# Two decoder layers on one core: the loop over layers written out, one weight tile split earlier, and the last norm writing its output directly

## The chip, the cores and the metric

One Trainium2 chip, of which the kernel uses one core. The metric is the device time of the whole program in microseconds. A core has five engines with their own instruction queues: TensorE (PE, matmuls, with weight loads shown apart as PEld), VectorE (DVE), ScalarE (ACT), GpSimd (POOL) and SyncE (SP), which here only issues transfers. They meet through semaphores.

## What is computed

Two layers of a causal decoder over 512 tokens of width 1024, all in float32. For each layer:

```
h = x @ w_in                       # split into three mixers and three gates
x = layer_norm(ALPHA * x + merged @ w_out)                     # norm 1
f_gate, f_up = split(x @ w_ffn_in)
ffn = (silu(f_gate) * f_up) @ w_ffn_out
ple = sigmoid(x @ w_ple_gate) * (p_i @ w_ple_proj)
x = layer_norm(ALPHA * x + ffn + ple)                          # norm 2
```

The mixers are sparse attention over the best 128 keys, latent attention, and a gated causal convolution of width 31. The result is x after the second layer.

## The kernel before

**Data.** Activations lie with features on the 128 partitions: `x` is eight blocks (`DK = 8`) of 128x512. To multiply in nearly full float32 precision, each operand is split into a high half (rounded to fp32r) and a low half (the rest), and each product is three matmuls: high by high, high by low, low by high (`three`, and the loop of `group`). The residual stream is kept as `xh` and `xl`.

**Weights.** Each layer's weights are 152 tiles (`TILES`) of 128x1024. SP loads tile t into `wraw` (two slots, `load`), ACT rounds it into `wh` (`high`, four slots, `WS`), POOL subtracts to make `wl` (`low`), and PE waits for `lo_ready` (`arrived`). SP may load a tile when the low half of the tile two before is made. ACT may write a slot of `wh` when PE has used the tile four before. ACT's queue is written out by hand: `high(n + LEAD)` with `LEAD = 3` stands beside the use of tile n, so that when a layer ends the first three tiles of the next one are split. The fourth (tile 3) is asked for at the head of the next pass of the layer loop, `high(n + LEAD, first)` at n = 0, that is behind everything that ACT does for norm 2. `weights` holds three tiles more than the two layers have, so that the last pass can load ahead as well; SP, ACT and POOL handle these three too.

**The layer loop.** ACT, PE, DVE and POOL each run `Fori(0, L)`, a hardware loop with the layer number in a register; semaphore counts that depend on it are worked out by register instructions. Within it stand shorter hardware loops (the 22 passes over the FFN's input tiles, for one).

**Norm 2 and the layer's end.** `norm` on DVE adds the last blocks, PE forms mean and mean square (L938, L946), ACT takes the root (`deviation`), and PE spreads the scale over the partitions (L950). Then, for each block j, DVE centres it (L1282) and scales it (L1306, signals `z_ready`); ACT adds the bias and rounds it into `xh` (`norm_high`, L579, signals `x_high`); DVE makes `xl` (L1312, signals `x_ready`). After norm 2 of either layer DVE also adds `xh` and `xl` back together into `u` (L1316, signals `z_full`). The next layer's first four tiles (group "idx", two blocks of x each, 24 matmuls each) start with `x_ready` of block 0. After the second layer, ACT sends `u` to `out` in four transfers of two blocks, each on `z_full`, behind its last `norm_high`.

Of the kernel before, what the change touches and what calls it, by code (L numbers as in the profile page):

```python
# [19 lines left out]
ALU = mybir.AluOpType  # L20
ACT = mybir.ActivationFunctionType
F32 = mybir.dt.float32
# [6 lines left out]
L = 2  # L29
NT = S // P  # L30
DK = D // P
# [46 lines left out]
T_PP = T_OUT + DK  # L78
T_PG = T_PP + 4
T_FI = T_PG + DK  # L80
T_FO = T_FI + 2 * FK
PARTS = -(-FK // DK)
TILES = T_FO + PARTS * DK
assert TILES % 4 == 0
TILE = 1024
LEAD = 3
WS = 4
# [135 lines left out]
def build(nc, x_t, ple_t, pos, freq, weights, params, out):  # L223
    with ExitStack() as ctx:
# [5 lines left out]
        def sem(name):  # L230
# [3 lines left out]
        xh = sb("xh", 0, [P, DK, S], F32R)  # L234
        xl = sb("xl", 16384, [P, DK, S], F32R)
        wraw = sb("wraw", 32768, [P, 2, TILE])
# [8 lines left out]
        par = sb("par", 78848, [P, NPAR])  # L245
        praw = sb("praw", 79680, [P, 2, S])
# [50 lines left out]
        u = sb("u", A0 + 90112, [P, DK, S])  # L297
# [26 lines left out]
        raw_loaded = [sem("raw_loaded0"), sem("raw_loaded1")]  # L324
        hi_ready, lo_ready, tile_used = sem("hi_ready"), sem("lo_ready"), sem("tile_used")
# [5 lines left out]
        par_loaded, ple_loaded, out_stored = sem("par_loaded"), sem("ple_loaded"), sem("out_stored")  # L331
# [26 lines left out]
        z_ready, x_high, x_ready, z_full = (  # L358
            sem("z_ready"), sem("x_high"), sem("x_ready"), sem("z_full"))
# [20 lines left out]
        def column(name, j):  # L380
            return par[:, PAR[name] + j:PAR[name] + j + 1]
# [4 lines left out]
        @block.sync  # L386
        def _(sp):
            for t in range(2):
                sp.dma_start(wraw[:, t, :], weights[t]).then_inc(raw_loaded[t], 16)
            def load(t, tile):  # L390

                sp.wait_ge(lo_ready, tile - 1)
                sp.dma_start(wraw[:, t, :], weights[bass.ds(tile, 1)].rearrange("a p n -> (a p) n")).then_inc(
                    raw_loaded[t], 16)

            with sp.Fori(1, L * TILES // 2 + 1) as m:
                for t in range(2):
                    load(t, m * 2 + t)
            sp.wait_ge(lo_ready, L * TILES + 1)
            sp.dma_start(wraw[:, 0, :], weights[L * TILES + 2]).then_inc(raw_loaded[0], 16)  # L400


        @block.gpsimd
        def _(pool):

            nc.gpsimd.memset(ident[:], 0.0).then_inc(zeroed, 1)
            nc.gpsimd.memset(causal[:], 0.0).then_inc(zeroed, 1)
            nc.gpsimd.memset(ones_d[:], 1.0 / D).then_inc(consts_ready, 1)
            nc.gpsimd.memset(ones_c[:], 1.0 / CC).then_inc(consts_ready, 1)
            nc.gpsimd.memset(ones_1[:], 1.0).then_inc(consts_ready, 1)  # L410
            nc.gpsimd.memset(eps_ln, LN_EPS).then_inc(consts_ready, 1)
            nc.gpsimd.memset(small[:, 64:72], 0.0).then_inc(consts_ready, 1)
            nc.gpsimd.memset(small[:, 76:128], 0.0).then_inc(consts_ready, 1)
            pool.wait_ge(zeroed, 2)
            nc.gpsimd.affine_select(out=ident[:], in_=ident[:], compare_op=ALU.not_equal, fill=1.0, base=0,
                                    pattern=[[-1, P]], channel_multiplier=1).then_inc(consts_ready, 1)
            nc.gpsimd.affine_select(out=causal[:, S - P:S], in_=causal[:, S - P:S], compare_op=ALU.is_ge, fill=NEG,
                                    base=0, pattern=[[-1, P]], channel_multiplier=1).then_inc(consts_ready, 1)

            def low(t, first):  # L420

                pool.wait_ge(hi_ready, first + (t + 1))  # L422
                nc.gpsimd.tensor_tensor(wl[:, t % WS, :], wraw[:, t % 2, :], wh[:, t % WS, :].bitcast(F32),  # L423
                                        ALU.subtract).then_inc(lo_ready, 1)

            for t in range(LEAD):
                low(t, 0)
            pool.sem_inc(passed, 1)
            with pool.Fori(0, L) as layer:
                first = layer * TILES  # L430
                with pool.Fori(0, T_PP // 4) as i:  # L431
                    for k in range(4):
                        low(LEAD + k, first + i * 4)
                with pool.Fori(0, (TILES - T_PP) // 4) as i:  # L434
                    for k in range(4):
                        low(T_PP + LEAD + k, first + i * 4)

        def logit(n):

# [4 lines left out]
        tile_group, t, col = {}, 0, {}  # L444
        for g, (name, ncol, nk, tiles) in enumerate(TOKEN_GROUPS):
# [4 lines left out]
            if t == T_CONV:  # L450
                t = T_U
# [4 lines left out]
        def _(act):  # L456
# [17 lines left out]
            def high(t, first):  # L474

                act.wait_ge(tile_used, first + (max(t - (WS - 1), 0) + START))
                act.wait_ge(raw_loaded[t % 2], first * 8 + 16 * (t // 2 + 1))
                nc.scalar.activation(wh[:, t % WS, :], wraw[:, t % 2, :], ACT.Copy).then_inc(hi_ready, 1)  # L478
# [98 lines left out]
            def norm_high(layer, n, j):  # L577
                act.wait_ge(z_ready, layer * 16 + (8 * n + j + 1))
                nc.scalar.activation(xh[:, j], u[:, j], ACT.Identity,  # L579
                                     bias=column(("l1b", "l2b")[n], j)).then_inc(x_high, 1)  # L580

            for t in range(LEAD):
                high(t, 0)
            with act.Fori(0, L) as layer:
                first = layer * TILES
                for kind, n in FRONT:
                    if kind == "tile":
                        high(n + LEAD, first)
                        if n == 1:

                            act.wait_ge(x_ready, layer * 16 + DK)
                            act.dma_start(par[:], params[bass.ds(layer, 1)].rearrange("a p n -> (a p) n")).then_inc(
                                par_loaded, 16)
                            act.dma_start(praw[:], ple_t[bass.ds(layer, 1)].rearrange("a p k n -> (a p) k n")).then_inc(
                                ple_loaded, 16)
                        if n in tile_group:
                            g, k = tile_group[n]
                            name, ncol, _, tiles = TOKEN_GROUPS[g]
# [6 lines left out]
                        elif CONV_PLACE[n][1] == 0:  # L605
                            j = CONV_PLACE[n][0]
# [59 lines left out]
                for q in range(12):  # L666
# [7 lines left out]
                    if q >= 8:  # L674
                        for c in range(2):
                            n = 2 * (q - 8) + c
# [40 lines left out]
                        nc.scalar.activation(hh[:, bass.ds(i * 2 + c, 1), :].rearrange("p a n -> p (a n)"),  # L717
                                             th[:, c, :], ACT.Copy, scale=0.5).then_inc(ffn_high, 1)
                for k in range(PARTS * DK):
                    high(T_FO + k + LEAD, first)  # L720
                    j = k // PARTS
                    if k % PARTS == 0 and j >= 4:
                        for jj in range(4) if j == 4 else range(j - 1, j):
                            squares(layer, 1, jj)
                squares(layer, 1, DK - 1)
                deviation(layer, 1)
                for j in range(DK):
                    norm_high(layer, 1, j)
            for j in range(0, DK, 2):
                act.wait_ge(z_full, (L - 1) * DK + j + 2)  # L730
                act.dma_start(out[:, j:j + 2], u[:, j:j + 2]).then_inc(out_stored, 16)
            act.wait_ge(out_stored, 16 * 4)


        @block.tensor
        def _(pe):
# [232 lines left out]
            pe.sem_inc(tile_used, START)  # L969
            pe.wait_ge(consts_ready, 8)  # L970
            pe.sem_inc(passed, 1)
            with pe.Fori(0, L) as layer:
                first = layer * TILES
                for kind, n in FRONT:
                    if kind == "scratch":
# [95 lines left out]
        def _(dve):  # L1071
# [152 lines left out]
            def norm(layer, n, start, tile):  # L1224
# [2 lines left out]


                x0, g, b = layer * 16 + 8 * n, ("l1g", "l2g")[n], ("l1b", "l2b")[n]
                total, squares = sums[n][:, 0], sums[n][:, 1]  # L1230

                def arrive(j):
# [66 lines left out]
                    center(j)  # L1299
                steps.wait()  # L1300
                dve.wait_ge(spread, layer * 2 + (n + 1))
                for j in range(DK + 2):
                    if j < DK:
                        if j >= EARLY:
                            steps.wait(back=min(EARLY - 1, DK - 1 - j))
                        v.scalar_tensor_tensor(u[:, j], u[:, j], column(g, j), scale, ALU.mult,  # L1306
                                               ALU.mult).then_inc(z_ready, 1)
                        if j + EARLY < DK:
                            center(j + EARLY)
                    if 1 <= j <= DK:  # L1310
                        dve.wait_ge(x_high, x0 + (DK + j))
                        v.scalar_tensor_tensor(xl[:, j - 1], u[:, j - 1], column(b, j - 1), xh[:, j - 1].bitcast(F32),  # L1312
                                               ALU.add, ALU.subtract).then_inc(x_ready, 1)
                    if n == 1 and j >= 2:
                        dve.wait_ge(x_ready, x0 + (DK + j - 1))
                        v.tensor_tensor(u[:, j - 2], xh[:, j - 2].bitcast(F32), xl[:, j - 2].bitcast(F32),  # L1316
                                        ALU.add).then_inc(z_full, 1)

            dve.sem_inc(passed, 1)
            with dve.Fori(0, L) as layer:  # L1320
                first = layer * TILES
                steps.stage(layer * V_LAYER)
                dve.wait_ge(par_loaded, layer * 16 + 16)
# [307 lines left out]
```

## Time and profile before

| what | value |
|---|---|
| median of three runs | 1975.85 us (1975.3 to 1978.69) |
| the profiled execution, its own time | 1980.51 us |
| its span, first to last instruction | 1978.7 us |
| mean granted TensorE clock | 0.979 |
| PE busy | 1873.0 us, 95% of the span |
| ACT, DVE, POOL busy | 37%, 51%, 38% |

Times in the trace are microseconds from the start of the span. PE's share of busy time counts matmuls that overlap in the pipeline, so it is no measure of how near PE is to its best, but where PE is idle the row says how long and for whom.

### The profile page before, as it was taken

The page shows a single profiled execution, that of the slowest core. Times are in us where ns is not written, and L with a number is a line of the kernel's source. Part 1 is how long each engine was busy: PE and PEld are TensorE (multiplying, and loading weights), DVE is VectorE, ACT ScalarE, POOL GpSimd, SP SyncE. Part 2 cuts the span into 40 slices and gives each one's busy share as a digit, 9 for nine tenths or more (in the row PEclk, how much of TensorE's full clock was granted, in tenths as well). Part 3 has the DMA queues.
Part 4 walks back from the last instruction along what each step waited for, and adds up shares of the span by engine and source line. Part 5 has one row for each costly group of instructions (what it writes and reads, how often), then busy time and mean ns, then how long its engine had stood idle before and what let it go on. Part 6 is the DMA issues. An engine that isn't in the chain of part 4 may idle for free.

```text
span 1978.7 us, 27887 instructions
## 1 busy us (share of the span) xinstructions
PE 1873.0 (95%) x9048; PEld 1551.4 (78%) x9048; DVE 1002.4 (51%) x1898; ACT 737.5 (37%) x1256; POOL 752.4 (38%) x321
## 2 busy tenths in 40 slices
PE   6999999999999999999999999999999899999995
PEld 5877878878777888887787878888777788888873
DVE  3269667748974111112353876676588721111025
ACT  3443455543342222222244435555433422222222
POOL 4433222234444444443443422222353534444441
PEclk9999999999999999999899999999999999999997
DMA  5222111112222222232232211111132222222322
GB/s 164 95 76 85 54 50 57 55 57 93 96 96 85 95 95 95 96 106 85 97 99 85 97 65 52 46 54 65 61 101 85 97 95 95 95 95 96 106 96 75
DMA packets 46334, 167.86 MB, mean 85 GB/s; under 512 B 5392, under 2 KB 5648, under 8 KB 46224
## 3 DMA queue, kind: packets, MB, share of 16 engines
q1 hardware_dynamic: 44208, 160.98, 24.6%
q10 hardware_dynamic: 2016, 5.47, 0.8%
q8 instruction: 62, 1.02, 0.2%
q14 instruction: 48, 0.39, 0.1%
HBM read 164.33 MB, written 2.10 MB: 84 GB/s over the span
## 4 chain that ended last, share of the span: by engine, by line
issue 68%; POOL 27%; PE 2%; DVE 1%; POOLq 1%; ACT 0%; DMA 0%; DVEq 0%; ACTq 0%
POOL sb_wl L423 27%; PE banks L741 1%; PE banks L739 1%; PE banks L740 1%; POOLq L422 0%; POOLq L434 0%; POOLq L431 0%; DVE sb_xl L1312 0%; DMA sb_rope_tmp<-in_freq 0%; DVE sb_u L1306 0%; ACT sb_xh L471 0%; DVE sb_u L1282 0%; PE banks L938 0%; PE banks L946 0%; PE banks L950 0%
## 5 line engine op out<-in xcount | busy, mean ns | idle before, releaser
L423 POOL TENSOR_TENSOR sb_wl<-sb_wraw,sb_wh 128x1024 fp32r<-128x1024 f32 x307 | 750.4, 2448 | 1194.1 <-ACT sb_wh L478 1193.8
L739 PE MATMUL banks<-sb_xh,sb_wh 128*128 128x512 f32 x1344 | 553.4, 412 | 12.2 <-DVE sb_u L1510 9.1
L741 PE MATMUL banks<-sb_xh,sb_wl 128*128 128x512 f32 x1344 | 529.0, 394 | 0.0
L740 PE MATMUL banks<-sb_xl,sb_wh 128*128 128x512 f32 x1344 | 528.7, 393 | 0.0
L478 ACT ACTIVATE sb_wh<-sb_wraw 128x1024 fp32r<-128x1024 f32 x307 | 323.2, 1055 | 271.0 <-PE banks L741 167.2
L739 PEld LDWEIGHTS banks<-sb_xh,sb_wh 128*128 128x128 f32 x1344 | 255.8, 190 | 62.4 <-POOL sb_wl L423 11.7
L741 PEld LDWEIGHTS banks<-sb_xh,sb_wl 128*128 128x128 f32 x1344 | 254.7, 190 | 54.8
L740 PEld LDWEIGHTS banks<-sb_xl,sb_wh 128*128 128x128 f32 x1344 | 256.2, 191 | 40.6
L1175 DVE SCALAR_TENSOR_TENSOR banks<-sb_hconv,sb_par,banks 128x512 f32<-128x512 f32 x232 | 173.8, 749 | 0.5
L739 PE MATMUL banks<-sb_hh,sb_wh 128*128 128x512 f32 x352 | 138.9, 395 | 1.6 <-POOL sb_wl L423 1.6
L741 PE MATMUL banks<-sb_hh,sb_wl 128*128 128x512 f32 x352 | 138.0, 392 | 0.0
L740 PE MATMUL banks<-sb_hl,sb_wh 128*128 128x512 f32 x352 | 137.4, 390 | 0.0
L1234 DVE TENSOR_TENSOR sb_u<-sb_u,banks 128x512 f32<-128x512 f32 x32 | 21.9, 686 | 198.8 <-PE banks L741 197.7
L1522 DVE TENSOR_TENSOR sb_th<-sb_th,banks 128x512 f32<-128x512 f32 x44 | 30.2, 687 | 181.3 <-PE banks L741 181.3
L783 PE MATMUL banks<-sb_wh,sb_xh 128*128 128x452 f32 (+3 forms) x256 | 91.5, 357 | 25.2 <-POOL sb_wl L423 21.8
L1519 DVE SCALAR_TENSOR_TENSOR sb_th<-sb_th,banks 128x512 f32<-128x512 f32 x44 | 30.3, 688 | 167.2 <-ACT sb_th L482 167.2
L523 ACT ACTIVATE sb_ptbuf<-banks 128x128 f32<-128x128 f32 (+3 forms) x128 | 55.8, 436 | 143.4 <-PE banks L839 143.3
L482 ACT ACTIVATE sb_th<-banks 128x512 f32<-128x512 f32 x60 | 35.9, 598 | 192.4 <-PE banks L741 192.1
L717 ACT ACTIVATE sb_hh<-sb_th 128x512 f32 x44 | 27.8, 632 | 207.7 <-DVE sb_th L1522 207.7
L784 PE MATMUL banks<-sb_wl,sb_xh 128*128 128x452 f32 (+3 forms) x256 | 90.9, 355 | 0.0
L785 PE MATMUL banks<-sb_wh,sb_xl 128*128 128x452 f32 (+3 forms) x256 | 90.6, 354 | 0.0
L739 PEld LDWEIGHTS banks<-sb_hh,sb_wh 128*128 128x128 f32 x352 | 66.1, 188 | 16.9 <-POOL sb_wl L423 2.5
(266 smaller groups left out, 2872.2 us busy)
## 6 DMA issues: line engine op xcount, KB each, us to landing
sb_wraw<-in_weights SPq DMA_DIRECT2D x307, 512.0 KB, 3.3
sb_u<-in_x ACTq DMA_DIRECT2D x4, 512.0 KB, 7.4
out<-sb_u ACTq DMA_DIRECT2D x4, 512.0 KB, 3.6
sb_praw<-in_ple ACTq DMA_DIRECT2D x2, 512.0 KB, 4.4
sb_par<-in_params ACTq DMA_DIRECT2D x2, 98.5 KB, 2.6
sb_rope_tmp<-in_freq ACTq DMA_DIRECT2D x1, 24.0 KB, 5.0
sb_small<-in_pos ACTq DMA_DIRECT2D x1, 2.0 KB, 3.8
```

Of the source, the lines that this page charges most:

```text
L423: nc.gpsimd.tensor_tensor(wl[:, t % WS, :], wraw[:, t % 2, :], wh[:, t % WS, :].bitcast(F32), ALU.subtract).then_inc(lo_ready, 1)
L478: nc.scalar.activation(wh[:, t % WS, :], wraw[:, t % 2, :], ACT.Copy).then_inc(hi_ready, 1)
L482: nc.scalar.activation(dst, psum[:, bank, :], ACT.Tanh, scale=0.5, bias=bias).then_inc(done, 1)
L523: nc.scalar.activation(ptbuf[:, n % 2, 0:w], psum[:, bank, 0:w], ACT.Copy).then_inc(turn_out, 1)
L739: nc.tensor.matmul(out, wh_, xh_, start=start, stop=False)
L740: nc.tensor.matmul(out, wh_, xl_, start=False, stop=False)
L741: return nc.tensor.matmul(out, wl_, xh_, start=False, stop=stop)
L783: nc.tensor.matmul(o, th_, h[:, kk], start=(k == 0), stop=False)
L784: nc.tensor.matmul(o, th_, lw[:, kk], start=False, stop=False)
L785: last = nc.tensor.matmul(o, tl_, h[:, kk], start=False, stop=(k == nk * tiles - 1))
L1175: steps.done(v.scalar_tensor_tensor(acc, h, w, acc, ALU.mult, ALU.add))
L1519: steps.done(v.scalar_tensor_tensor(tc, tc, 1.0, psum[:, 4 + 2 * c, :], ALU.add, ALU.mult))
```

## The change

Four things. The layer loop of ACT, PE and DVE becomes a Python loop, so its body stands twice in each engine's program with constants in place of the register; POOL runs one flat loop over all tiles. At the end of layer 0, `high` of the next layer's tile 3 is issued between `deviation` and the eight `norm_high`, and dropped at n = 0 of layer 1. The three tiles past the end are no longer loaded nor split. In norm 2, L1316 is gone from both layers; in the last layer L1312 is gone too, and ACT's Identity adds the bias and writes the float32 value straight to `u`, each block signals `z_full`, and SP (no longer ACT) sends each block by itself, eight transfers of 256 KB.

```diff
@@ sync
-            with sp.Fori(1, L * TILES // 2 + 1) as m:
+            with sp.Fori(1, L * TILES // 2) as m:
                 for t in range(2):
                     load(t, m * 2 + t)
-            sp.wait_ge(lo_ready, L * TILES + 1)
-            sp.dma_start(wraw[:, 0, :], weights[L * TILES + 2]).then_inc(raw_loaded[0], 16)
+            for j in range(DK):
+                sp.wait_ge(z_full, j + 1)
+                sp.dma_start(out[:, j], u[:, j]).then_inc(out_stored, 16)
+            sp.wait_ge(out_stored, 16 * DK)
@@ gpsimd
-            for t in range(LEAD):
-                low(t, 0)
             pool.sem_inc(passed, 1)
-            with pool.Fori(0, L) as layer:
-                first = layer * TILES
-                with pool.Fori(0, T_PP // 4) as i:
-                    for k in range(4):
-                        low(LEAD + k, first + i * 4)
-                with pool.Fori(0, (TILES - T_PP) // 4) as i:
-                    for k in range(4):
-                        low(T_PP + LEAD + k, first + i * 4)
+            with pool.Fori(0, L * TILES // WS) as i:
+                for k in range(WS):
+                    low(k, i * WS)
@@ scalar
-            with act.Fori(0, L) as layer:
+            for layer in range(L):
                 first = layer * TILES
                 for kind, n in FRONT:
                     if kind == "tile":
-                        high(n + LEAD, first)
+                        if layer == 0 or n > 0:
+                            high(n + LEAD, first)
...
                 for k in range(PARTS * DK):
-                    high(T_FO + k + LEAD, first)
+                    if T_FO + k + LEAD < TILES or layer < L - 1:
+                        high(T_FO + k + LEAD, first)
...
                 deviation(layer, 1)
-                for j in range(DK):
-                    norm_high(layer, 1, j)
-            for j in range(0, DK, 2):
-                act.wait_ge(z_full, (L - 1) * DK + j + 2)
-                act.dma_start(out[:, j:j + 2], u[:, j:j + 2]).then_inc(out_stored, 16)
-            act.wait_ge(out_stored, 16 * 4)
+                if layer < L - 1:
+                    high(LEAD, first + TILES)
+                    for j in range(DK):
+                        norm_high(layer, 1, j)
+                else:
+                    for j in range(DK):
+                        act.wait_ge(z_ready, layer * 16 + (DK + j + 1))
+                        nc.scalar.activation(u[:, j], u[:, j], ACT.Identity,
+                                             bias=column("l2b", j)).then_inc(z_full, 1)
@@ tensor
-            with pe.Fori(0, L) as layer:
+            for layer in range(L):
@@ vector, norm
+                last = n == 1 and layer == L - 1
-                for j in range(DK + 2):
+                for j in range(DK + 1):
...
-                    if 1 <= j <= DK:
+                    if 1 <= j <= DK and not last:
                         dve.wait_ge(x_high, x0 + (DK + j))
...
-                    if n == 1 and j >= 2:
-                        dve.wait_ge(x_ready, x0 + (DK + j - 1))
-                        v.tensor_tensor(u[:, j - 2], xh[:, j - 2].bitcast(F32), xl[:, j - 2].bitcast(F32),
-                                        ALU.add).then_inc(z_full, 1)
@@ vector
-            with dve.Fori(0, L) as layer:
+            for layer in range(L):
@@ kernel
-    tiles = np.concatenate([tiles, tiles[:LEAD]], axis=0)
```

## Rows read from the trace of the kernel before

**Rows 1.** The page: span and instructions of all queues, and each engine's busy time.
```profile
span 1978.7 us, 27887 instructions
PE 1873.0 (95%) x9048; PEld 1551.4 (78%) x9048; DVE 1002.4 (51%) x1898; ACT 737.5 (37%) x1256; POOL 752.4 (38%) x321
```

**Rows 2.** Waits of PE: engine, tile, line <- releaser: us in total, times, longest.
```profile
PE banks L783 <- POOL sb_wl L423: 21.8, 2, 18.4
PE banks L839 <- DVE sb_ystage L1160: 16.2, 20, 1.4
...
PE banks L811 <- DVE sb_cl L1354: 6.7, 2, 3.4
```

**Rows 3.** Timeline of ACT, the layer boundary: start, us, what [idle before <- releaser].
```profile
983.87 0.72 ACT L579 ACTIVATE sb_xh<-sb_u,sb_par 128x512 fp32r<-128x512 f32 x1 [3.96 <-DVE sb_u L1306]
...
1001.72 1.28 ACT L478 ACT_TABLE_LOAD   x1 [1.95 <-issue]
...
1003.02 2.00 ACT L478 ACTIVATE sb_wh<-sb_wraw 128x1024 fp32r<-128x1024 f32 x2
```

**Rows 4.** Timeline of PE at the boundary, around tile 3's start and end.
```profile
1002.99 0.36 PE L785 MATMUL banks<-sb_wh,sb_xl 128*128 128x452 f32 x1
1006.71 0.47 PE L783 MATMUL banks<-sb_wh,sb_xh 128*128 128x452 f32 x1 [3.36 <-POOL sb_wl L423]
...
1012.71 0.37 PE L783 MATMUL banks<-sb_wh,sb_xh 128*128 128x452 f32 x1
...
1013.32 0.35 PE L783 MATMUL banks<-sb_wh,sb_xh 128*128 128x416 f32 x1
```

**Rows 5.** Stretches: length, busy us (x instructions) by engine, PEclk, DMA share, GB/s.
```profile
991.00:1003.00 12.00, 12.00 (x61) 10.99 (x59) 11.15 (x18) 4.18 (x5) 0.00 (x0) 1.00 0.01 2
1008.20:1011.20 3.00, 3.00 (x9) 2.63 (x9) 0.00 (x0) 0.21 (x1) 0.72 (x1) 0.50 0.79 264
103.00:110.00 7.00, 5.79 (x16) 4.74 (x17) 3.62 (x6) 1.63 (x2) 2.37 (x1) 0.52 0.01 2
1076.80:1083.80 7.00, 5.83 (x28) 4.82 (x28) 3.54 (x6) 1.64 (x2) 2.39 (x1) 1.00 0.01 2
```

**Rows 6.** Timeline of all engines, norm 2 of layer 0, its DVE steps.
```profile
980.15 0.69 DVE L1294 TENSOR_TENSOR sb_sums<-sb_ident,sb_small 128x512 f32<-128x512 f32 x1
...
985.61 0.75 DVE L1312 SCALAR_TENSOR_TENSOR sb_xl<-sb_u,sb_par,sb_xh 128x512 fp32r<-128x512 f32 x1
```

**Rows 7.** Timelines of ACT, POOL and DVE in norm 1 of layer 0.
```profile
546.69 1.04 ACT L478 ACTIVATE sb_wh<-sb_wraw 128x1024 fp32r<-128x1024 f32 x1
...
547.81 2.36 POOL L423 TENSOR_TENSOR sb_wl<-sb_wraw,sb_wh 128x1024 fp32r<-128x1024 f32 x1 [6.45 <-ACT sb_wh L478]
...
555.54 2.03 DVE L1312 SCALAR_TENSOR_TENSOR sb_xl<-sb_u,sb_par,sb_xh 128x512 fp32r<-128x512 f32 x1
```

**Rows 8.** Timeline of DVE and ACT, last layer's norm 2.
```profile
1955.62 0.75 DVE L1306 SCALAR_TENSOR_TENSOR sb_u<-sb_u,sb_par,banks 128x512 f32<-128x512 f32 x1 [0.54 <-PE banks L950]
...
1961.32 0.74 DVE L1306 SCALAR_TENSOR_TENSOR sb_u<-sb_u,sb_par,banks 128x512 f32<-128x512 f32 x1
1961.98 0.68 DVE L1282 TENSOR_TENSOR sb_u<-sb_u,banks 128x512 f32<-128x512 f32 x1
...
1962.58 0.74 DVE L1312 SCALAR_TENSOR_TENSOR sb_xl<-sb_u,sb_par,sb_xh 128x512 fp32r<-128x512 f32 x1
...
1963.84 0.74 DVE L1306 SCALAR_TENSOR_TENSOR sb_u<-sb_u,sb_par,banks 128x512 f32<-128x512 f32 x1
```

**Rows 9.** Timeline of DVE, the last pieces.
```profile
1973.39 1.28 DVE L1316 TENSOR_TENSOR sb_u<-sb_xh,sb_xl 128x512 f32<-128x512 f32 x2
```

**Rows 10.** The source view of the output transfers, L731.
```profile
L731 ACTq DMA_DIRECT2D out<-sb_u x4: 338/404/557, 1971.7 to 1974.7; - x4
...
DMA to landing us min/median/max: 2.7/3.6/4.3
```

**Rows 11.** The DMA view from 1970 us to the end, rate in 40 equal slices.
```profile
GB/s 0 0 0 0 0 0 0 0 0 0 0 255 400 400 364 455 400 364 437 400 400 419 346 437 419 419 382 400 401 419 437 400 364 455 146 0 0 0 0 0
```

More of the change, by code:

```diff
@@ L587, in _ @@
                     if kind == "tile":
-                        high(n + LEAD, first)
+                        if layer == 0 or n > 0:
+                            high(n + LEAD, first)
                         if n == 1:
                             act.wait_ge(x_ready, layer * 16 + DK)
-                            act.dma_start(par[:], params[bass.ds(layer, 1)].rearrange("a p n -> (a p) n")).then_inc(
+                            act.dma_start(par[:], params[layer]).then_inc(
                                 par_loaded, 16)
-                            act.dma_start(praw[:], ple_t[bass.ds(layer, 1)].rearrange("a p k n -> (a p) k n")).then_inc(
+                            act.dma_start(praw[:], ple_t[layer]).then_inc(
                                 ple_loaded, 16)
```

## The prediction

> **What bounds the kernel now.** I read the page first [rows 1]: PE is busy for 1873.0 of 1978.7 us. The change takes nothing from PE's work, so it can only win where PE is idle or after PE has ended. The view of waits shows who keeps PE idle [rows 2]. The line to see is PE L783 waiting for POOL's low half, 21.8 us in two waits: one of 18.4 us is the start of the program, which the change leaves alone; the other is 3.4 us. I then looked at two places in the timelines, the layer boundary and the end.
>
> At the boundary, PE starts layer 1 when DVE has made block 0 of `xl` at 985.61 + 0.75 = 986.36 us [rows 6], and then runs without a gap through tiles 0 to 2 (61 matmuls in 12 us, clock 1.00, the faster of its two levels, 2.4 GHz) [rows 5]. Tile 3 is not there: its first matmul is at 1006.71, 3.72 us after the one before [rows 4]. ACT is why. It has ended its last `norm_high` at 1001.72 - 1.95 = 999.77, is then 1.95 us idle for nothing but issue (the head of the loop), loads a table for 1.28 us, and only at 1003.02 rounds tile 3 [rows 3]; POOL's low half of it comes after that, and PE's idle time ends with it [rows 4]. Behind the gap PE's granted clock is 0.50 (1.2 GHz) in the stretch 1008.2 to 1011.2, where only 9 matmuls pass in 3 us [rows 5].
>
> At the end PE has nothing left once it has spread the scale, and from 1955.62 on the last 23 us are one chain on DVE, then the transfers: scale, centre, `xl`, and the sum back into `u` for each block, 2.52 us a block (scale at 1961.32, the next at 1963.84) [rows 8]. The last sum ends at 1973.39 + 1.28 = 1974.67, ACT issues the last transfer right behind it (L731's last start is 1974.7), and it takes about 3.6 us to land; 0.4 us of closing remain to 1978.7 [rows 9, 10]. ACT's first transfer could not leave before 1971.7, as it stands behind the last `norm_high`, so 2 MB go out at about 400 GB/s in 5.2 us: the queue is full from the first issue to the end [rows 11].
>
> **Part 1: tile 3 split ahead of the norm's high halves.** The moved instructions are one `high` of 1.06 us (L478) on ACT and, through it, one `low` of 2.4 us on POOL (2.36 at 547.81 [rows 7]), and SP's load of tile 5, which waits for that low half. The edit takes them past the eight `norm_high` in ACT's queue; POOL has nothing else in its queue and SP only the later loads, which come earlier too. ACT is idle for 3.96 us between the root and block 0's `norm_high` (979.91 to 983.87) [rows 3]. The `high` would run from about 979.9 to 980.9, POOL from 980.95 to 983.35. Even with a table load of 1.28 us ahead of it ACT would be free at 982.3, so nothing behind it is late. Its own waits are met: the slot is free when the down projection has ended, and the raw tile has been there since before the norm. Norm 1 already has this order and shows it: `high` at 546.69 behind the root, with no table load between, `low` at 547.81 [rows 7]. PE then finds tile 3 ready at 1003.2.
>
> What PE gains: it passes from tile 2's last start (1002.99) to tile 4's first (1013.32) in 10.33 us [rows 4]. At the pitch of the full clock, 0.203 us (three steps from 1012.71 to 1013.32), these 25 steps take 5.1 us. The gain is 5.2 us: 3.5 us of idle time and 1.7 us that the half clock costs. What is late next? Tile 4: after the last `norm_high` (now near 996.8, since DVE drops L1316, 0.60 us a block [rows 8]) ACT rounds it at once, and POOL has it by about 1000.2, 8 us before PE asks at 1008.1. Block 7 of `xl` is there by 997.6, wanted after 1005. So no new wait, 5.2 us stay.
>
> The neighbour that speaks against it is POOL beside DVE. L1312, with two inputs in SBUF, takes 0.74 us alone and 2.03 us where a `low` ran beside it (555.54) [rows 6, 7]. At the boundary the only such instruction near the moved `low` is L1294, at 980.15 to 980.84; the `low` comes in 0.1 us after it ends, and 0.8 us after it has begun. The first L1312 is at 985.61, 2.2 us after the `low` [rows 6]. I charge nothing; were the `low` to start first and L1294 to wait for the whole of it, all that follows would be 2.4 us later and part 1 worth 2.8 us. The Trainium skill (SBUF — State Buffer, section SBUF: two separate sides) says that GpSimd and a VectorE instruction with two SBUF inputs take a shared port pair in turn, the first to start for its whole length; the rows of norm 1 agree. By that rule the order of the two starts decides between the two sums, and as they start now it is the first.
>
> **Part 2: the end.** On DVE, per block, the 0.66 us from L1312's start to L1316's and the 0.60 us from there to the next scale go, 1962.58 to 1963.84. What stays is 0.66 us from scale to centre and 0.60 from the centre to what follows, 1.26 us (1961.32 to 1962.58) [rows 8]. Scale 0 starts at 1955.62 as now; scale 6 at 1955.62 + 6 x 1.26 = 1963.18; scale 7 follows 0.66 us later at 1963.84 and ends at 1964.58. ACT's Identity (0.72 us, as L579 [rows 3]; f32 output, taken as equal) ends at 1965.33 and keeps up, 0.72 in 1.26. SP, free since its last load, issues within 0.04 us. Landing of 256 KB is not in the trace. Above it lies the fastest 512 KB transfer, 2.7 us [rows 10]; below it that less 256 KB at 400 GB/s [rows 11], 2.1 us. The transfers are 1.26 us apart, more than the 0.65 us each needs at 400 GB/s, so they don't queue unless 2 KB rows go at half the rate; then one takes 1.3 us and the last is late by about 0.3 us. I take 2.3 us. The end is 1965.37 + 2.3 + 0.4 = 1968.1, a gain of 10.6 us, between 9.9 and 10.8. The Trainium skill (DMA: Bandwidth & Descriptors, section Anatomy of one DMA) gives 2.0 us plus the bytes at 436 GB/s for a transfer of another path; as an estimate that is 2.6 us here and a gain of 10.3 us, and no run so far shows a transfer of this size.
>
> **Part 3: the layers written out, three tiles fewer.** The loop head's 1.95 us and table load on ACT are in part 1. The three extra tiles are split beside down-projection matmuls that don't wait for them: nothing. The page counts 27,887 instructions, 21,571 of them in the busy rows [rows 1]; the other 6,300 are register, semaphore, branch and issue instructions, and most of the register ones go. They mostly run while their engine is busy with the instruction before. They can count only where PE waits on another engine's reply: 20 waits on L1160 of 0.8 us, above all [rows 2]. If none is on such a path the gain is 0; the trace's rows don't price a register step, so from above I take a quarter of the 16.2 us of those 20 waits, 4 us. I take 1 us, nearer to nothing, since the steps in [rows 8] follow one another before the one ahead has fully ended, with no room for a register step between them. Twice as much program as a body is the same instructions streamed as now, since each layer passes through its body once.
>
> **Sum.** 5.2 + 10.6 + 1.0 = 16.8 us: the profiled execution of 1980.51 us (span 1978.7 and 1.8 around it) would become 1963.7. The median of the runs is 4.7 us under the profiled one; with the same 16.8 us off it is 1959.0. A measurement of this kernel can tell about 0.2%, 4 us, from no change.
>
> **Rivals.**
> - *The clock takes some of it back.* PE's granted clock after a gap isn't steady: an idle time of 3.4 us before L811, once in each layer (6.7 us in two), is followed by half clock in layer 0 (16 matmuls in 7 us) and by full clock in layer 1 (28) [rows 2, 5]. Everything in layer 1 moves by 5 us, so that gap may fall the other way: 12 matmuls x 0.25 us (7 / 28) = 3.0 us lost, giving 1962.0, or half that if only the boundary's 1.7 us stay. It can win as much elsewhere. Chance 0.15.
> - *POOL holds DVE at the boundary*, as above: 2.4 us, 1961.4. The margin of 0.8 us speaks against it. Chance 0.04.
> - *The boundary edit does nothing for the time*: tile 4 or the parameter transfer becomes the late one and takes the place of tile 3. Then 10.6 + 1 stay: 1964.2. POOL's 2.4 us a tile against PE's 4.9 speaks against it. Chance 0.04.
> - *The register instructions count in full*: 3 us more, 1956. Chance 0.10.
> - *Slower*: instruction fetch of the written-out program. A jump to code that isn't at hand costs ACT 1.95 us [rows 3]. If the straight program stalled PE like that at the borders of fetched blocks, 9 such stalls (17.6 us) eat the gain, from 11 on it is slower by 0.2%, and 12 give 1982.4. Against it: the body is already this straight, and 61 matmuls pass without a gap [rows 5]. Chance 0.05, of which 0.02 for 7 to 10 stalls, within 0.2%.
>
> The forecast has the other 0.62, with its own range 1957 to 1961.5. Range for 8 in 10: 1954.5 (register gain in full and a kinder clock) to 1965 (boundary edit void, transfers at the slow bound). Faster by over 0.2%: 0.95; within: 0.02; slower: 0.03.
>
> **What would show it.** Part 1: L478 between L575 and the first L579, one `low` before 984 us, no idle on PE L783 for POOL but the start's, no half clock near 1008 us; tile 4's first matmul near 1008.1 us. Part 2: L1306 at 1.26 us pitch, the last transfer 9.7 us after the first L1306, the span's end about 12.5 us after it instead of 23.1. Part 3: PE's waits on L1160 a little shorter. It is wrong if PE shows a new wait near tile 4, if L1294 or L1312 takes over 2 us there, or if PE gets short gaps that no engine explains.

## The result, and the profile after

The changed kernel takes 1967.09 us (median of five runs, 1966.31 to 1967.98), the kernel before 1975.85 us in the same job (five runs, 1975.16 to 1979.2): ratio 0.995, interval 0.9937 to 0.9962. It is faster by 8.8 us where 16.8 were forecast, and it lies above the range. The profiled execution took 1966.31 us; its span is 14.2 us shorter than that of [rows 1]. The page:

```profile
span 1964.5 us, 25834 instructions
PE 1874.9 (95%) x9048; PEld 1553.1 (79%) x9048; DVE 992.2 (51%) x1874; ACT 730.1 (37%) x1250; POOL 745.6 (38%) x318
```

PE has as many matmuls as before and is busy 1.9 us longer. The waits of PE (as [rows 2]):

```profile
PE banks L783 <- POOL sb_wl L425: 18.1, 1, 18.1
PE banks L839 <- DVE sb_ystage L1160: 14.5, 20, 1.3
...
PE banks L811 <- DVE sb_cl L1351: 6.9, 2, 3.4
```

L783 waits for POOL once, at the start; the 3.4 us wait at the boundary is gone. The 20 waits on L1160 are 1.7 us shorter together. Further down, two waits of 1.5 us before L783 now have no releaser ("issue", 3.1 us in two); in the kernel before the same two stand as waits for ACT (3.0 us in two), so they are no new gaps.

**The boundary**, as [rows 3] and [rows 6]. Timeline of ACT:

```profile
978.80 0.30 ACT L570 ACTIVATE sb_small<-sb_small 128x4 f32<-128x4 f32 x1 [0.85 <-DVE sb_small L1291]
979.00 1.04 ACT L473 ACTIVATE sb_wh<-sb_wraw 128x1024 fp32r<-128x1024 f32 x1
982.97 0.72 ACT L574 ACTIVATE sb_xh<-sb_u,sb_par 128x512 fp32r<-128x512 f32 x1 [2.92 <-DVE sb_u L1307]
...
995.13 0.72 ACT L574 ACTIVATE sb_xh<-sb_u,sb_par 128x512 fp32r<-128x512 f32 x1 [0.60 <-DVE sb_u L1307]
995.76 1.05 ACT L473 ACTIVATE sb_wh<-sb_wraw 128x1024 fp32r<-128x1024 f32 x1
```

Timelines of DVE, POOL and PE, and PE's stretch over tiles 2 to 4:

```profile
979.34 0.69 DVE L1295 TENSOR_TENSOR sb_sums<-sb_ident,sb_small 128x512 f32<-128x512 f32 x1
...
984.70 0.74 DVE L1313 SCALAR_TENSOR_TENSOR sb_xl<-sb_u,sb_par,sb_xh 128x512 fp32r<-128x512 f32 x1
```

```profile
980.12 2.35 POOL L425 TENSOR_TENSOR sb_wl<-sb_wraw,sb_wh 128x1024 fp32r<-128x1024 f32 x1 [5.63 <-ACT sb_wh L473]
996.89 4.76 POOL L425 TENSOR_TENSOR sb_wl<-sb_wraw,sb_wh 128x1024 fp32r<-128x1024 f32 x2 [14.42 <-ACT sb_wh L473]
```

```profile
985.59 0.71 PE L783 MATMUL banks<-sb_wh,sb_xh 128*128 128x452 f32 x1 [3.52 <-DVE sb_xl L1313]
```

```profile
1001.00:1007.00 6.00, 6.00 (x31) 5.51 (x30) 0.00 (x0) 1.06 (x1) 2.87 (x2) 1.00 0.53 167
```

ACT rounds tile 3 right behind the root, without a table load, and tile 4 with no gap behind its last `norm_high`. POOL makes the low half just after L1295 has ended, and both DVE instructions keep their 0.7 us. PE runs through at the faster clock, with no idle time and no half clock at 1008.

**The end**, as [rows 8] to [rows 10]. Timelines of DVE, then ACT, then SP's queue, and the source view of the transfers:

```profile
1952.38 0.75 DVE L1307 SCALAR_TENSOR_TENSOR sb_u<-sb_u,sb_par,banks 128x512 f32<-128x512 f32 x1 [0.55 <-PE banks L950]
1953.05 0.68 DVE L1283 TENSOR_TENSOR sb_u<-sb_u,banks 128x512 f32<-128x512 f32 x1
1953.64 0.74 DVE L1307 SCALAR_TENSOR_TENSOR sb_u<-sb_u,sb_par,banks 128x512 f32<-128x512 f32 x1
...
1959.92 1.40 DVE L1307 SCALAR_TENSOR_TENSOR sb_u<-sb_u,sb_par,banks 128x512 f32<-128x512 f32 x2
```

```profile
1953.16 0.72 ACT L731 ACTIVATE sb_u<-sb_u,sb_par 128x512 f32<-128x512 f32 x1 [3.97 <-DVE sb_u L1307]
...
1960.70 1.38 ACT L731 ACTIVATE sb_u<-sb_u,sb_par 128x512 f32<-128x512 f32 x2 [0.53 <-DVE sb_u L1307]
```

```profile
L401 SPq DMA_DIRECT2D out<-sb_u x8: 332/332/349, 1953.9 to 1962.1; - x8
...
DMA to landing us min/median/max: 2.0/2.0/2.1
```

The scales are 1.26 us apart, as forecast, and the Identity takes 0.72. A transfer of 256 KB lands in 2.0 us where the prediction took 2.3. From the first scale to the end of the span it is 12.1 us, from 23.1.

**Where it came back.** So each mended place gained what it should. Part of the time was lost where nothing was changed: in norm 1, and behind the gap at L811. As [rows 5], first 12 us around norm 1 of layer 1 in the kernel before, then the same in the changed one and 7 us from the gap at L811 of its layer 1:

```profile
1514.00:1526.00 12.00, 10.09 (x43) 7.30 (x42) 8.23 (x16) 4.84 (x8) 2.56 (x2) 0.86 0.27 89
```

```profile
1508.00:1520.00 12.00, 10.50 (x37) 7.21 (x36) 6.32 (x12) 3.36 (x5) 3.39 (x2) 0.72 0.24 70
1071.00:1078.00 7.00, 5.81 (x21) 4.82 (x22) 3.59 (x6) 1.63 (x2) 2.39 (x1) 0.76 0.00 0
```

PE's timeline of the changed kernel at both places shows what half clock (1.2 GHz) is:

```profile
1072.19 0.93 PE L811 MATMUL banks<-sb_ident,sb_h_ckv 128*128 128x128 f32 x4 [3.42 <-DVE sb_cl L1351]
...
1073.35 0.63 PE L740 MATMUL banks<-sb_xl,sb_wh 128*128 128x512 f32 x1
1073.77 0.63 PE L741 MATMUL banks<-sb_xh,sb_wl 128*128 128x512 f32 x1
...
1511.37 2.39 PE L938 MATMUL banks<-sb_ones_d,sb_sums 128*128 128x1 f32 x16 [1.50 <-DVE sb_sums L1271]
...
1515.90 0.63 PE L740 MATMUL banks<-sb_pl,sb_wh 128*128 128x512 f32 x1
1516.33 0.63 PE L741 MATMUL banks<-sb_ph,sb_wl 128*128 128x512 f32 x1
```

The matmuls stand 0.42 us apart instead of 0.23, though the idle times ahead of them are no longer than before (3.4 us at L811 in both kernels, 1.5 us at norm 1 of layer 1 where it was 1.9). I laid the two traces side by side by the number of the matmul (both kernels have the same 9048 in the same order) and took the time from one to another:

| between matmuls | where | before | after |
|---|---|---|---|
| 96 to 2668 | layer 0 up to norm 1 | 505.88 | 505.21 |
| 2668 to 2677 | norm 1, layer 0 | 2.05 | 3.56 |
| 2677 to 4512 | layer 0 behind norm 1 | 430.04 | 429.50 |
| 4512 to 4524 | norm 2, layer 0 | 8.95 | 8.13 |
| 4524 to 4620 | layer 1, tiles 0 to 3 | 26.92 | 21.96 |
| 4700 to 5000 | around L811, layer 1 | 57.59 | 59.14 |
| 5300 to 7182 | attention and output, layer 1 | 378.05 | 376.71 |
| 7182 to 7208 | norm 1, layer 1 | 6.08 | 7.58 |
| 7208 to 9000 | layer 1 behind norm 1 | 417.99 | 418.53 |
| last matmul to the end | | 24.26 | 13.32 |

Two norms and L811 give back 1.5 + 1.5 + 1.6 = 4.6 us.

### The profile page after: what moved, and what is told of

Same layout as the page of the kernel before. It is cut to its first block, busy times and chain, and to the rows that moved or that the text cites. A ratio compares the mean times of both kernels' runs of the same rounds, so it can differ in the third digit from the quotient of the medians.

```text
span 1964.5 us, 25834 instructions
## 1 busy us (share of the span) xinstructions
PE 1874.9 (95%) x9048; PEld 1553.1 (79%) x9048; DVE 992.2 (51%) x1874; ACT 730.1 (37%) x1250; POOL 745.6 (38%) x318
## 4 chain that ended last, share of the span: by engine, by line
issue 68%; POOL 28%; PE 2%; POOLq 1%; DVE 0%; ACT 0%; DVEq 0%
POOL sb_wl L425 28%; PE banks L739 1%; PE banks L741 1%; PE banks L740 1%; POOLq L424 0%; POOLq L429 0%; DVE sb_u L1307 0%; DVE sb_u L1283 0%; PE banks L938 0%; PE banks L946 0%; PE banks L950 0%; POOLq L425 0%; ACT sb_u L731 0%; DVE sb_sums L1271 0%; DVE sb_u L1235 0%
## 5 line engine op out<-in xcount | busy, mean ns | idle before, releaser
L783 PE MATMUL banks<-sb_wh,sb_xh 128*128 128x452 f32 (+3 forms) x256 | 90.8, 355 | 21.6 <-POOL sb_wl L425 18.1
```

The costliest lines, as they stand in the source:

```text
L783: nc.tensor.matmul(o, th_, h[:, kk], start=(k == 0), stop=False)
```

## The experiments

Times are medians; "before" is that of the same job. The kernel before was run 66 times in all, with e1: 1973.96 to 1983.1, median 1978.0, mean 1977.9; the changed one 11 times with e5: 1963.7 to 1968.1, mean 1966.5. So the gain over many executions is near 11.4 us; the two jobs that hold both kernels gave 8.8 and 14.6.

**e1: the kernel before, unchanged.** For the spread of one program.

> The kernel before, unchanged, for more executions and another profile. Theory A (the profiled execution of before was one of its long ones, about 5 us over its usual time, and the sum was made against it): most executions at 1975 to 1976 and some at 1979 to 1980, the profile of a short one shows PE's pass over the boundary (tile 2's last start to tile 4's first) at 10.3 us as before and the missing 4 to 5 us somewhere in the middle, in stretches of half clock. Theory B (a part is worth less in the usual executions than in the profiled one): the pass over the boundary is shorter than 10.3 us, or the end after the first scale shorter than 23.1 us, in the short executions.

1976.06 us (12 runs, 1973.96 to 1982.14), before 1978.15, ratio 0.9992 [0.9981, 1.0002]. Its profiled span is 1974.8 us, 3.9 under [rows 1] for the same program, and the matmul-by-matmul comparison puts it in four places: norm 1 of layer 1 (6.08 to 4.59 us), 0.40 just ahead of it, 1.0 behind, and 1.14 in the last norm. The pass over the boundary (26.99 us) and the end (24.26) are as in the first trace, as Theory A expected. Its stretch there:

```profile
1514.00:1526.00 12.00, 10.49 (x51) 7.94 (x50) 9.71 (x19) 6.64 (x11) 2.95 (x2) 1.00 0.26 88
```

Clock 1.00 where the first trace had 0.86 and the changed kernel 0.72. The 0.40 are no clock: PE waited 1.9 us for the sums of norm 1 in the first trace and 1.5 here. The other 3.6 are where the half clock falls. The recorded clocks say the same of the runs that were not profiled: of 61 executions of this kernel, the 10 with a mean clock of 0.979 took 1981.9 us on average, the 23 with 0.982 took 1975.2.

**e2, e3, e4: one part at a time.** e2 only writes the layers out; e3 adds the boundary edit; e4 is e2 with the end's edits (L1316 gone from both layers, the last layer written by blocks) but without the move.

```diff
# e2
-            with act.Fori(0, L) as layer:
+            for layer in range(L):
# the same for PE and DVE
# e3 = e2 and
-                        high(n + LEAD, first)
+                        if layer == 0 or n > 0:
+                            high(n + LEAD, first)
...
+                if layer < L - 1:
+                    high(LEAD, first + TILES)
```

> Only the layer loops of ACT, PE and DVE written out; order, last norm, transfers and POOL's loops as before. The prediction's part 3 says 1 us faster, 1974.9. Theory A with a price for writing out (half clock falls differently, or fetch): 1979 to 1981, about 4 to 5 us slower than before. Theory B: 1974 to 1976.

> Written out as in the run before this one, and tile 3 of the next layer split ahead of the norm's high halves; last norm and transfers as before. Both theories take the difference to the written-out kernel: prediction 5.2 us less, 1969.7; Theory A: 5 us less than the written-out kernel, so 1975 to 1976, no gain over before; Theory B, boundary worth less: within 2 us of the written-out kernel.

> Written out, and the last norm writes full values and is sent block by block by SP; the sum back into u is gone from both layers; tile 3 stays behind the norm's high halves. Prediction: 10.6 us less than the written-out kernel, 1964.3. Theory A: also 10.6 us less than it, so 1969 to 1971. Theory B, end worth less: 6 us less than it or fewer.

e2: 1978.06 us (11 runs, 1970.47 to 1979.51), ratio 0.9994 [0.9981, 1.0008]. e3: 1977.42 (12, 1973.6 to 1979.27), 0.9993 [0.9982, 1.0004]. e4: 1965.96 (6, 1963.08 to 1968.15), 0.9937 [0.9922, 0.9951]; before 1978.15. e2 lies between what its two theories expected, e3 at 0.6 us under e2 where 5 were expected by Theory A (Theory B had named under 2, because the boundary would be worth less, which e3's trace below does not bear out), and e4 at 12.1 us under e2 where 10.6 were. By the medians the written-out loop and the boundary edit are worth nothing, and all of the gain is e4's edits'. Yet in e3's trace the boundary is 5.3 us shorter (tiles 0 to 3: 21.58 us for 26.92), and norm 1 of layer 1 takes 7.75 us for 6.08. The same is seen in e2 (7.85) and e4 (7.64). Already e2 mends most of the boundary; ACT there:

```profile
999.65 0.72 ACT L579 ACTIVATE sb_xh<-sb_u,sb_par 128x512 fp32r<-128x512 f32 x1 [1.20 <-DVE sb_u L1306]
1000.28 1.99 ACT L478 ACTIVATE sb_wh<-sb_wraw 128x1024 fp32r<-128x1024 f32 x2
```

Written out, ACT has neither the 1.95 us of the loop head nor the table load of 1.28 us of [rows 3] between the last `norm_high` and tile 3. Tile 3 starts 17.9 us behind layer 1's first matmul instead of 20.3, and PE's gap there is 1.4 us instead of 3.4. L1316 has a second part in what is left: with it in place POOL's low half of tile 3, which starts beside DVE's last sums, takes 3.57 us in e2 (3.54 in e9 below), and without it 2.40 in e4. That is the prediction's neighbour the other way round, POOL slowed beside a DVE instruction with two SBUF inputs.

**e5, e6: the changed kernel again, and with tile 3 left where it was** (behind the `norm_high`).

```diff
-                        if layer == 0 or n > 0:
-                            high(n + LEAD, first)
+                        high(n + LEAD, first)
...
-                    high(LEAD, first + TILES)
```

> The changed kernel, unchanged, beside the same executions of before as the three runs below. If the 1975.85 of before was a lucky small sample, the difference of the medians is 11 us; if not, 8 to 9 us as first measured.

> The changed kernel with tile 3 split behind the norm's high halves again, as in before. The prediction charges the move with the whole 5.2 us of the boundary: this would be 1972. The traces of the parts say that the loop head, the table load and the sum back into u alone made tile 3 late, and all three are gone anyway: then this is within 1 us of the changed kernel, and PE has no gap at tile 3.

e5: 1966.07 us, 0.9928 [0.9916, 0.994]; e6: 1967.45, 0.9932 [0.992, 0.9944]; before 1980.71. ACT in e6:

```profile
997.50 0.73 ACT L574 ACTIVATE sb_xh<-sb_u,sb_par 128x512 fp32r<-128x512 f32 x1 [0.59 <-DVE sb_u L1305]
998.13 1.04 ACT L473 ACTIVATE sb_wh<-sb_wraw 128x1024 fp32r<-128x1024 f32 x1
```

PE has no idle time there between 987.96 and 1010 us and its time for tiles 0 to 3 is 21.27 us. With the loop written out and L1316 gone, ACT is done with norm 2 early enough for tile 3 where it was: the move isn't needed. That is what was expected, and not the 1972 of the prediction's reading. e5's expectation named 11 us if the first sample of before was a lucky one, and 8 to 9 if not; its job gave 14.6.

**e7, e8: the clock held up.** To take the clock out of the comparison, that is to keep it at its faster level, PE gets work that nobody reads in the places where it waits: transposes of `ident` into a bank that is free there, 147 in each layer, in the kernel before (e7) and in the changed one (e8).

```diff
+            def keep(bank, n):
+                for _ in range(n):
+                    nc.tensor.transpose(psum[:, bank, 0:P], ident[:], ident[:])
# 26 ahead of L811's wait, 22 ahead of the first scores, 15 ahead of
# the sums of each norm, 9 more in norm 2, 34 behind norm 2, 26 ahead of the FFN
```

> The kernel before with transposes of the identity into a free PSUM bank issued by PE in its idle stretches (ahead of the fourth low half of the normed c, of the first score, of the norm's sums and spread, behind norm 2 and ahead of the FFN), about 130 a layer, nothing else changed. Clock theory (stretches of half clock behind PE's idle times cost both kernels some 8 to 14 us, and a different share in each execution): fewer stretches of half clock, 5 to 12 us faster than before, a narrower spread than 1974 to 1983. Rival (the clock is not what parts the executions): within 2 us of before, same spread, or slower by the fillers' length.

> The changed kernel with the same fillers. Clock theory (the change's steps give about 18 us: boundary 5, end 11, register steps 2, and moved stretches of half clock take 6 to 8 of them back): 16 to 18 us under the filled kernel before. Rival (the written-out program costs 5 us or more by fetch or otherwise): 10 to 12 us under it, as without fillers.

e7: 1960.98 us, 0.991 [0.9894, 0.9925]; e8: 1941.0, 0.9806 [0.9793, 0.9818]; before 1980.71. Both gained more than was expected: e7 is 19.7 us under before where 5 to 12 were named, and e8 is 20.0 under e7 where 16 to 18 were. e7's five runs lie between 1960.17 and 1961.18 but for one of 1966.59, whose mean clock is 0.993 where the others have 0.995 and 0.996. The rows of 100 to 1930 us, of before, after, e7 and e8 in this order, have the clock ahead of the DMA share:

```profile
100.00:1930.00 1830.00, 1767.97 (x8521) 1459.72 (x8520) 943.42 (x1794) 681.94 (x1168) 697.58 (x286) 0.99 0.25 83
```

```profile
100.00:1930.00 1830.00, 1772.64 (x8532) 1463.57 (x8531) 945.89 (x1787) 678.85 (x1166) 699.96 (x286) 0.98 0.26 83
```

```profile
100.00:1930.00 1830.00, 1792.46 (x8843) 1487.14 (x8842) 954.93 (x1799) 685.96 (x1173) 705.78 (x289) 1.00 0.25 84
```

```profile
100.00:1930.00 1830.00, 1798.62 (x8889) 1491.56 (x8887) 954.43 (x1802) 682.46 (x1172) 700.31 (x286) 1.00 0.26 83
```

The two figures of 1.00 are rounded: one short stretch of half clock is left in either trace, in e8 in norm 1 of layer 0 (2.72 us there, 1.84 in e12 below), in e7 behind a wait of 1.5 us in layer 1:

```profile
1090.00:1096.00 6.00, 5.75 (x37) 5.76 (x38) 5.69 (x17) 1.06 (x2) 2.38 (x1) 0.72 0.22 66
```

The fillers also move PE's start of layer 1 in e7: its jump to the loop head comes behind the 34 fillers, and PE starts 2.00 us after them, though block 0 of `xl` (made from 976.03 on) would have allowed it at 976.8. Timeline of PE in e7:

```profile
973.23 3.87 PE L739 MATMUL banks<-sb_ident 128*128 128x128 f32 x34
979.10 0.47 PE L787 MATMUL banks<-sb_wh,sb_xh 128*128 128x452 f32 x1 [2.00 <-DVE sb_xl L1325]
```

Norm 2 takes 9.55 us there and 7.37 in e8. e9's expectation counts this as a cost of the fillers, but it costs nothing: PE then waits for tile 3 anyway, 2.96 us, and tile 3's time is set by ACT (which rounds it at 993.44, behind its own loop head and table load) and POOL. Its first matmul comes 20.3 us behind block 0 of `xl` in e7, and 20.4 in the kernel before, where PE started at once.

So the parts with the clock held up are best read from the traces of e7 and e12 (the changed kernel without the move, below; its PE has no half clock while it is busy). The spans differ by 19.5 us: norm 2 and tiles 0 to 3 of layer 1 together 5.4 (32.52 to 27.11), the end 10.9 (23.78 to 12.85), attention of layer 0 1.6, e7's leftover half clock 1.6; the rest cancels out. Without the leftover 17.9 us are the change's, against 16.8 of the sum and near 11.4 with the clock free. e8 is also the fastest kernel: 25.5 us below the changed one although it issues 294 more matmuls. That fits an estimate from the changed kernel's trace: its clock records show half clock during 56 us of PE's busy time, of which half, 28 us, is lost.

**e9 to e12: the parts with the clock held up.** e9, e10 and e11 are e2, e3 and e4 with the fillers, e12 is e6 with them. e9 also tries the rival of instruction fetch with nothing else in its way.

> The layer loops written out, nothing else, with the fillers. The filled kernel before took 1961.0, of which 2.3 us are the fillers' own (PE's jump to the loop's head now comes behind them). Parts at a held clock: the jump's 2.3, 2.2 to 2.7 us of PE's 3.2 us gap at tile 3 (loop head and table load on ACT gone), about 2 us of register steps: 1954 to 1955. If writing out costs time by itself: 1958 or more.

> As the run before, and tile 3 split ahead of the norm's high halves, with the fillers. The prediction's whole boundary gain as the move's own: 5 us less than written out alone. The traces so far: only the last 0.5 to 1 us of the gap at tile 3 is left for it: 0.5 to 1 us less.

> Written out, the last norm's full values sent block by block, the sum back into u gone, with the fillers. At a held clock: 10.9 us for the end and the same 0.5 to 1 us at tile 3, since the norm's high halves end 3 us earlier without the sum: 11.5 to 12 us less than written out alone, 1942 to 1943. If the end is worth 10.6 us and no more, 10.6 us less.

> The changed kernel with tile 3 split behind the high halves again, with the fillers: the move alone, in the final kernel. Same as the filled changed kernel, 1941.0 within 0.5 us, if the move has nothing left to win; 1944 to 1946 if it has the gap.

| kernel | median us (range) | ratio to before, 1977.06 |
|---|---|---|
| e9, written out | 1956.06 (1955.1 to 1958.73) | 0.989 [0.9873, 0.9907] |
| e10, and boundary | 1952.11 (1951.76 to 1954.94) | 0.9876 [0.9858, 0.9894] |
| e11, e9 and end | 1941.49 (1941.01 to 1943.13) | 0.9819 [0.9805, 0.9834] |
| e12, e8 without the move | 1941.12 (1940.8 to 1941.49) | 0.9817 [0.9802, 0.9831] |

e9 is 4.9 us under e7. Its profiled execution is its longest (1958.73), 2.0 under e7's: 1.6 in attention of layer 0 and 1.6 of e7's leftover half clock are gained, 0.4 lost at the boundary, where e9 has half clock and e7 has not. Nothing in this pair looks like a fetch stall. e10 is 4.0 us under e9, and 5.9 at the boundary in the traces (tiles 0 to 3: 25.59 to 19.73 us); 0.5 to 1 were expected. In e9 the boundary still has its gap and its half clock, in e10 neither; timeline of PE and stretch of e9, then the stretch of e10:

```profile
993.86 0.75 PE L787 MATMUL banks<-sb_wh,sb_xh 128*128 128x452 f32 x1 [2.92 <-POOL sb_wl L423]
```

```profile
990.00:1000.00 10.00, 7.08 (x22) 5.98 (x21) 3.13 (x4) 2.19 (x3) 6.53 (x3) 0.66 0.54 169
```

```profile
990.00:1000.00 10.00, 10.00 (x52) 9.51 (x51) 2.57 (x3) 3.87 (x6) 7.49 (x3) 1.00 0.55 169
```

(The gap is 2.92 us although the loop is written out. Tile 3 comes 18.1 us behind block 0 of `xl` in e9 as in e2, but at full clock PE is through tiles 0 to 2 in 14.6 us where e2 took 16.2.) e11 is 14.6 us under e9, where 11.5 to 12 were expected: 10.8 at the end (last matmul to the end 23.62 to 12.86 us) and the boundary as in e10, without the move. In the traces of e10 and e11 PE has no half clock while it is busy, so their medians price the end by themselves: 10.6 us. e12 and e8, which differ by the move alone, are 0.1 us apart, as expected.

## Why the prediction was off

- **Part 1, 5.2 us.** Right in size: tiles 0 to 3 take 4.96 us less in the profiled pair, and 5.4 together with norm 2 with the clock held up (e7 to e12). "POOL holds DVE" did not come: L1295 0.69 us, L1313 0.74. But the cause was put too narrowly. The move alone is worth nothing in the finished kernel (e6 with e5, ratios 0.0004 apart, and e12 with e8): the written-out loop and L1316's going do its work. In the traces with fillers tile 3 starts 20.3 us behind block 0 of `xl` in e7, 18.1 with the loop written out (e9), and 15.0, with no gap, where either the move (e10) or L1316's going (e11, e12) is added. The prediction put the loop head's 3.2 us and the dropped L1316 beside the move and never asked whether they would do.
- **Part 2, 10.6 us.** Right: 24.26 to 13.32 us, 10.9. The landing was mis-sized by 0.3 us (2.0, not 2.3). The estimate of 2.6 us by the Trainium skill's figure for a transfer of another path (DMA: Bandwidth & Descriptors, section Anatomy of one DMA) is further from the row.
- **Part 3, 1.0 us.** About right: with the clock held (e7 to e12) attention and what lies around it is 1.6 us shorter in layer 0 (501.87 to 500.27) and unchanged in layer 1, and the two stretches behind norm 1 are 0.3 us longer each. Without the fillers attention is 2.0 us shorter over both layers. The chance of 0.10 for 3 us more is not borne out.
- **Tile 4, transfers, fetch.** No new wait; e9, faster than e7, speaks against the fetch rival.
- **The step that failed** is the one from the sum to the time: "The median of the runs is 4.7 us under the profiled one; with the same 16.8 us off it is 1959.0." The forecast is 8.1 us too low, and the numbers say how. (a) In the profiled pair 14.2 us came, 2.6 fewer than 16.8. The clock took 4.6 and other small losses 0.8, while the gains were 2.8 more than forecast: 1.0 in attention, 0.8 in norm 2 of layer 0 (the clock again, this time in favour), 0.5 behind norm 1 of layer 0, 0.3 each at the start and the end, and 0.2 less at the boundary. (b) 4.7 us are the difference between the profiled execution before, 1980.51 us, and the median of its job, 1975.85. By e1's trace and the recorded clocks this is for the most part where the half clock fell in either: e1's span differs by 3.9 from the first one, 3.6 of it for that reason. A sum made on one execution was taken off the level of others, and that level was itself low: 1975.85 is the median of five, 1978.0 that of all 66. Against all runs the gain is 11.4 us, 5.4 short of the sum and not 8.1. (c) 0.8 us is the changed kernel's median above its profiled execution. 2.6 + 4.7 + 0.8 = 8.1.
- **The rival that came** is "the clock takes some of it back", priced at 3.0 us with 0.15. It named the right place (L811, layer 1) at 12 matmuls x 0.25 us = 3.0; the row shows 21 matmuls where layer 1 had 28 and 1.6 us lost. It missed norm 1, where 1.5 us in each layer went; in layer 1 every written-out kernel without fillers has it (7.57 to 7.85 us). The idle time that norm 1 starts with stood in the view of PE's waits of the kernel before, in a row that the prediction passed over:

```profile
PE banks L938 <- DVE sb_sums L1270: 6.4, 4, 1.9
```

The clock was looked at only behind the two gaps of 3.4 us.

That the clock, and not something else, is the cause is shown by e7 to e12: with it held, the whole change comes to 17.9 us and its parts to their sizes (5.4 for the boundary with norm 2, 10.6 to 10.9 at the end), and with it free (e3) 5.3 us seen at the boundary leave under 1 us in the median. The Trainium skill (TensorE: Matmul & The Clock Gate, section What's actually happening) says that a monitor sets the clock by how busy the engine was just before; the rows agree, 0.98 without and 1.00 with the fillers. What stays open is why a shift of some us in the program puts more half clock into norm 1: no run moved norm 1 alone.

## What to carry to other kernels

- In a kernel with many short waits of PE, price every change twice: what it takes away, and what the clock does behind the waits that stay. A profile is one draw: take sums against several executions, and widen the range by their spread.
- Before costing a move, ask what the other edits of the same change already free. Here the loop head and a dropped add did all of it.
- Idle PE can be filled: 294 transposes that nobody reads took 25.5 us off the changed kernel (1966.5 to 1941.0).

## What the runs showed of the hardware

- Whether half clock follows an idle time of 1.5 to 3.5 us can't be told from the gap alone: the 3.4 us gap before L811 in layer 1 was followed by full clock in the kernel before [rows 5] and in e1, and by half clock in the changed one; the gap at tile 3 by full clock in e7 (2.96 us) and by half clock in e9 (2.92).
- The spread of one program (1973.96 to 1983.1 us, 0.46%) is wider than what parts 1 and 3 bring together; with the fillers the changed kernel spreads over 2.9 us (e8, five runs) and its twin without the move over 0.7 (e12, five runs).
- The turn of the layer's hardware loop shows on ACT as 1.95 us without work and a table load of 1.28 us [rows 3], and on PE, where fillers stand ahead of it, as 2.0 us of idle time (e7); written out, neither is there (e2, e9).
- DVE and POOL slow each other both ways: L1312 took 2.03 us beside a low half and 0.74 alone [rows 6, 7]; the low half of tile 3 took 3.54 to 3.57 us beside DVE's last sums (e2, e9) and 2.40 without them (e4, e12).
